# Gate and branch projections of a transformer layer as seven block products each, with tokens on the rows

## The reference

```python
h = rms_norm(x, norm1_g) * (1.0 + sc1) + sh1            # 256 x 1024
q1, q2, k1, k2, va, qs, ks, vs, ga, gb = split(h @ w_in)  # ga, gb: the last 2 x 1024 columns
oa = differential_attention(...)                        # 8 heads, normed per head
ob = stick_breaking_attention(...)                      # 16 heads of 64
merged = sigmoid(ga) * (oa @ w_pa) + sigmoid(gb) * (ob @ w_pb)
x = x + g1 * (merged @ w_o)
# then: norm, router, top 4 of 32 experts (SwiGLU, 1024 wide), final norm
```

## Time and profile before

| | |
|---|---|
| median of 3 runs | 1316.11 us |
| profiled execution, whole | 1315.63 us |
| its span in the trace | 1313.9 us |
| PE busy, share of the span | 1264.5 us, 96% |
| DVE busy | 551.4 us, 42% |
| ACT busy | 178.1 us, 14% |
| HBM read | 476.10 MB, 363 GB/s over the span |
| granted clock of PE, mean | 0.997 |

### The profile page before, as it was taken

One profiled execution on the slowest core, in us unless ns is written; L12 is line 12 of the kernel. 1 busy time (PEld: TensorE's weight loads), 2 busy tenths in 40 slices (PEclk: granted clock), 3 DMA queues, 4 the chain that ended last, 5 costly groups with the idle time before them and its releaser, 6 DMA issues.

```text
span 1313.9 us, 16916 instructions
## 1 busy us (share of the span) xinstructions
PE 1264.5 (96%) x5985; PEld 583.5 (44%) x5986; DVE 551.4 (42%) x1232; ACT 178.1 (14%) x378; POOL 12.6 (1%) x31
## 2 busy tenths in 40 slices
PE   6999999999999999999999999999999999899997
PEld 4867867888653333333333333333333333333332
DVE  3354695332253444434333343334344343334344
ACT  2102323320020110001100000001000111011002
POOL 0000000100000000000000000000000000000000
PEclk9999999999999999999999999999999999999999
DMA  9967665238669999999999999999999999799995
GB/s 354 331 248 273 246 236 203 77 128 324 256 228 413 430 429 427 428 430 427 428 430 428 428 429 429 427 428 429 410 430 427 427 430 428 315 429 430 429 427 208
DMA packets 59183, 477.55 MB, mean 363 GB/s; under 512 B 4991, under 2 KB 5076, under 8 KB 32532
## 3 DMA queue, kind: packets, MB, share of 16 engines
q1 hardware_dynamic: 58852, 476.11, 88.1%
q10 hardware_dynamic: 304, 1.06, 0.2%
HBM read 476.10 MB, written 1.05 MB: 363 GB/s over the span
## 4 chain that ended last, share of the span: by engine, by line
PE 75%; DMA 18%; DVE 4%; issue 1%; SPq 1%; ACT 0%; DVEq 0%
PE bank L1748 25%; DMA down_ring<-in_w_down 17%; PE bank L1787 15%; PE bank L1387 11%; PE bank L1580 4%; PE bank L1422 4%; PE bank L1736 3%; PE bank L1714 3%; PE bank L1636 2%; PE bank L1706 2%; PE bank L1478 1%; DMA down_ring<-in_w_ada 1%; DVE scratch L1208 1%; DVE scratch L1206 1%; DVE scratch L839 1%
## 5 line engine op out<-in xcount | busy, mean ns | idle before, releaser
L1748 PE MATMUL bank<-gu_ring,scratch 128*64 128x512 f32 x2048 | 459.3, 595 | 0.4 <-DVE scratch L1133 0.4
L1748 PEld LDWEIGHTS bank<-gu_ring,scratch 128*64 128x64 f32 x2048 | 143.3, 137 | 283.5 <-issue 283.2
L1787 PE MATMUL bank<-down_ring,scratch 128*64 128x512 f32 x1024 | 235.5, 602 | 23.0 <-DMA down_ring<-in_w_down 17.9
L1387 PE MATMUL bank<-gu_ring 128*128 128x256 f32 x640 | 143.8, 381 | 0.0
L1787 PEld LDWEIGHTS bank<-down_ring,scratch 128*64 128x64 f32 x1024 | 71.0, 137 | 145.4 <-issue 133.5
L1387 PEld LDWEIGHTS bank<-gu_ring 128*128 128x128 f32 x640 | 119.8, 190 | 20.3 <-issue 4.0
L1196 DVE TENSOR_TENSOR scratch<-bank,bgu 128x512 f32<-128x512 f32 x32 | 22.1, 691 | 219.1 <-PE bank L1714 219.1
L735 ACT ACTIVATE scratch<-bank 128x512 f32<-128x512 f32 x32 | 19.1, 597 | 683.2 <-PE bank L1748 683.2
L1164 DVE TENSOR_TENSOR xres<-xres,bank 128x512 f32<-128x512 f32 x132 | 81.8, 682 | 57.7 <-PE bank L1736 57.7
L1714 PEld LDWEIGHTS bank<-ident,scratch 128*128 128x128 f32 x392 | 41.0, 140 | 80.2 <-issue 26.7
L1132 DVE TENSOR_TENSOR scratch<-bank,a 128x256 f32<-128x256 f32 x66 | 27.8, 421 | 114.1 <-PE bank L1714 114.1
(11 more groups left out here) (271 smaller groups left out, 844.9 us busy)
## 6 DMA issues: line engine op xcount, KB each, us to landing
gu_ring<-in_w_gu SPq DMA_DIRECT2D x128, 2048.0 KB, 23.5
down_ring<-in_w_down SPq DMA_DIRECT2D x64, 2048.0 KB, 17.3
gu_ring<-in_w_in SPq DMA_DIRECT2D x32, 1024.0 KB, 8.5
gu_ring<-in_w_ada SPq DMA_DIRECT2D x16, 1024.0 KB, 7.1
down_ring<-in_w_ada SPq DMA_DIRECT2D x8, 512.0 KB, 10.5
gu_ring<-in_w_ada SPq DMA_DIRECT2D x8, 512.0 KB, 11.4
gu_ring<-in_w_pa SPq DMA_DIRECT2D x4, 1024.0 KB, 6.3
gu_ring<-in_w_pb SPq DMA_DIRECT2D x4, 1024.0 KB, 6.2
```

The costliest lines, as they stand in the source:

```text
L1387: last = M(dst[:, b * T:(b + 1) * T], group_chunk(group, kt // 4)[:, kt % 4, cols], hT[:, kt, :], start=kt == 0, stop=kt == KT - 1)
L1748: last = M(bank[f // 2][64 * a:64 * a + 64, :], xT[:, kt % 4, kt // 4, :], gu_ring[:, 8 * half + kt, f * 512:(f + 1) * 512], start=kt == 0 ...
L1787: last = M(bank[7][64 * a:64 * a + 64, :], act_sb[:, kt % 4, kt // 4, :], down_ring[:, kt // 2, (kt % 2) * D + a * 512:(kt % 2) * D + (a + ...
```

## The change

The four products are each made of seven block products, as the values are. `matrix(m, n)` is product `n` of matrix `m` (0 and 1 the gates, 2 and 3 the branches): 4 matmuls of 128 tokens by 512 columns. There are now 28 steps on PE, step `s` being `matrix(s // 7, s % 7)`, each followed by `stick_breaking(s)` while `s` is below 18. The results have the tokens on the rows. Sums of weight quarters (`sum_matrix`, four of 128x2048 for each matrix), sums of the left side for `oa` and `ob` (`sum_left`, four of 128x512 each; those of `h` are kept), and the additions of the products (`add_matrix`, five of 128x512 for each matrix) are written by hand into DVE's list between the `weigh` of the heads. ACT copies four blocks of each matrix from PSUM (`matrix_copy`) and applies the sigmoid later in place. The merged rows are turned by PE (`transpose_merged`, 8 transposes for each 128 tokens) and copied by ACT to `mergedT` before `mix`.

Product `n` waits for its sums, for copies that free its bank and for additions that have read it; the waits that matter are in the diff. On SP, both groups of a matrix come free together at its last product, and the loads for expert 1 into slots 8 to 15 come later and in another order.

```diff
-                    load_gu(1, 1, 0)
...
                 if j == 2:
-                    sp.wait_ge(merged_ready, 4)
-                    for pair in (2, 3):
-                        load_gu(1, 1, pair)
+                    sp.wait_ge(merged_ready, 2)
+                    load_gu(1, 1, 3)
+                    load_gu(1, 1, 0)
+                    sp.wait_ge(rowsT_done, 6)
+                    load_gu(1, 1, 2)
...
+            def matrix_copy(m, n):
+                act.wait_ge(product_done, 12 + 6 * m + (1, 3, 4, 4)[n])
...
+            def sum_matrix(m, n):
...
+                    last = V.tensor_tensor(first_sum[m], group_chunk(right, 0), group_chunk(left, 0), ALU.subtract)
+                elif n == 1:
...
+                    last = V.tensor_tensor(group_chunk(left, 0), group_chunk(right, 1), first_sum[m], ALU.subtract)
...
+            sum_matrix(0, 0)
+            dve.wait_ge(later_ready, 1)
+            weigh(0)
+            weigh(1)
+            add_matrix(0, 0)
...
+            sum_matrix(0, 1)
+            weigh(2)
+            weigh(3)
+            dve.wait_ge(root_ready, 2)
             own.then(V.reciprocal(osq[:], osq[:]))
             V.tensor_tensor(oav, oav, ...).then_inc(oa_ready, 1)
...
+            sum_matrix(0, 2)
+            add_matrix(0, 1)
+            add_matrix(0, 2)
+            weigh(4)
+            weigh(5)
+            obT_copy(0)
+            sum_matrix(0, 3)
+            add_matrix(0, 3)
+            weigh(6)
+            weigh(7)
+            obT_copy(1)
+            add_matrix(0, 4)
+            sum_matrix(1, 0)
+            add_matrix(1, 0)
+            weigh(8)
+            weigh(9)
+            obT_copy(2)
+            sum_matrix(1, 1)
+            sum_matrix(1, 2)
+            weigh(10)
+            weigh(11)
+            obT_copy(3)
+            add_matrix(1, 1)
+            sum_matrix(1, 3)
+            add_matrix(1, 2)
+            add_matrix(1, 3)
+            weigh(12)
+            weigh(13)
+            obT_copy(4)
+            add_matrix(1, 4)
+            sum_left(oaT)
+            sum_matrix(2, 0)
+            weigh(14)
+            weigh(15)
+            obT_copy(5)
+            obT_copy(6)
+            add_matrix(2, 0)
...
+            def matrix(m, n):
...
+                if n == 0:
+                    wait_group(pe, left, 0)
+                    if m == 0:
+                        pe.wait_ge(emptied, EMPTIED_HT + TURN_OAT)
+                        pe.wait_ge(parts_added, 6)
+                    elif m < 3:
+                        pe.wait_ge(parts_added, 10 + 5 * m)
+                    else:
+                        pe.wait_ge(obT_ready, SBH // 2)
...
+                if n == 2:
+                    pe.wait_ge(right_sums_ready, 8 + 4 * m + 1)
+                    if m < 3:
+                        pe.wait_ge(parts_added, 10 + 5 * m + 1)
...
+                if n == 3:
+                    pe.wait_ge(right_sums_ready, 8 + 4 * m + 2)
+                    pe.wait_ge(m_copied, 4 * m + 1)
...
+                if n == 6:
+                    pe.wait_ge(right_sums_ready, 8 + 4 * m + 4)
+                    pe.wait_ge(parts_added, 10 + 5 * m + 4)
+                for k in range(4):
+                    done = M(bank[into[m == 3]][:, :], rows_[:, k, :], cols[:, k, :], start=first and k == 0,
+                             stop=last and k == 3, skip_group_check=True)
...
+            for s in range(28):
+                if s == 5:
                     pe.wait_ge(oa_ready, 1)
+                    pe.wait_ge(parts_added, 13)
+                    transpose_oa(0)
...
+                if s == 27:
+                    pe.wait_ge(emptied, EMPTIED_HT + TURN_MERGED)
+                    transpose_merged(0)
+                matrix(s // 7, s % 7)
```

More of the change, by code:

```diff
@@ L612, in empty @@
                 branch, n = g // 6, g % 6
[L613 to L621, removed]
+                src = bank[(4, 6)[h] if g == 1 else turn % 2][:, :]
+                dst = qkT[:, branch, 4 * n + 2 * h:4 * n + 2 * h + 2, :].rearrange("p b t -> p (b t)")
+                A(dst, src, ACT.Copy, scale=DH ** -0.5 if n < 2 else 1.0).then_inc(emptied, 1)
             def differential(s):
@@ L673, in turned @@
                 A(sb_a[:, h % 3, :], bank[2 + h % 4][:, 0:384], ACT.Copy).then_inc(sbaT_ready, 1)
[L675 to L690, removed]
+            def matrix_copy(m, n):
+                act.wait_ge(product_done, 12 + 6 * m + (1, 3, 4, 4)[n])
+                tt, half = ((0, 0), (1, 1), (0, 1), (1, 0))[n]
+                A(gate_and_branch[m][:, tt, half * CW:(half + 1) * CW], bank[((0, 1, 0, 0), (2, 3, 2, 2))[m == 3][n]][:, :],
+                  ACT.Copy).then_inc(m_copied, 1)
@@ new lines, in gate_sigmoid, with oaT_copy @@
+            def gate_sigmoid(m, tt):
+                act.wait_ge(parts_added, 10 + 5 * m + 5)
+                A(gate_and_branch[m][:, tt, :], gate_and_branch[m][:, tt, :], ACT.Sigmoid).then_inc(sigmoid_ready, 1)
+            def oaT_copy(n):
+                act.wait_ge(rowsT_done, n + 1)
+                A(oaT[:, 2 * n:2 * n + 2, :].rearrange("p k t -> p (k t)"), bank[1][:, :], ACT.Copy,
+                  scale=nsub[:, 0:1]).then_inc(emptied, 1)
+            for s in range(28):
+                for n in {0: (0,), 2: (1,), 3: (2, 3)}.get(s % 7, ()):
+                    matrix_copy(s // 7, n)
+                for n in {5: (0, 1), 6: (2, 3)}.get(s, ()):
+                    oaT_copy(n)
+                if s in (8, 9, 15, 16):
+                    gate_sigmoid(s // 15, (s // 15 + s) % 2)
+                if s == 20:
@@ L699, in _ @@
                     keep_and_stop(s + 1)
+            for tt in range(TT):
+                for a in range(2):
+                    act.wait_ge(rowsT_done, 5 + tt)
+                    A(mergedT[:, 4 * a:4 * a + 4, tt * P:(tt + 1) * P],
+                      bank[(6, 4)[tt] + a][:, :].rearrange("p (k t) -> p k t", k=4), ACT.Copy).then_inc(emptied, 1)
             for tt in range(TT):
@@ new lines, in add_matrix @@
+            def add_matrix(m, n):
+                tt, half = ((0, 0), (1, 1), (0, 1), (1, 1), (1, 0))[n]
+                dst = gate_and_branch[m][:, tt, half * CW:(half + 1) * CW]
+                if n == 0:
+                    dve.wait_ge(product_done, 12 + 6 * m + 2)
+                    dve.wait_ge(m_copied, 4 * m + 1)
+                    other = bank[4 if m == 3 else 1][:, :]
+                elif n == 1:
+                    dve.wait_ge(m_copied, 4 * m + 3)
+                    other = gate_and_branch[m][:, 0, CW:2 * CW]
+                elif n == 2:
+                    dve.wait_ge(product_done, 12 + 6 * m + 5)
+                    dve.wait_ge(parts_added, 10 + 5 * m + 2)
+                    other = bank[3 if m == 3 else 1][:, :]
+                elif n == 3:
+                    dve.wait_ge(product_done, 12 + 6 * m + 6)
+                    dve.wait_ge(parts_added, 10 + 5 * m + 2)
+                    other = bank[5 if m == 3 else 0][:, :]
+                else:
+                    dve.wait_ge(filled, 2 * LAST_FILL[m] + 2)
+                    dve.wait_ge(m_copied, 4 * m + 4)
+                    other = bank[5 if m == 3 else 0][:, :]
+                V.tensor_tensor(dst, dst, other, ALU.add).then_inc(parts_added, 1)
@@ new lines, in obT_copy, with merge @@
+            def obT_copy(n):
+                dve.wait_ge(sbpv_done, 2 * n + 2)
+                V.tensor_copy(obT[:, n, :], bank[6 + n % 2][:, 0:T]).then_inc(obT_ready, 1)
+            def merge(n):
+                tt, half = ((0, 0), (0, 1), (1, 1), (1, 0))[n]
+                cols = slice(half * CW, (half + 1) * CW)
+                gate_b, branch_b, merged = gate_and_branch[1], gate_and_branch[3], gate_and_branch[0]
+                dve.wait_ge(parts_added, 25 + (1, 3, 4, 5)[n])
+                own.then(V.tensor_tensor(branch_b[:, tt, cols], branch_b[:, tt, cols], gate_b[:, tt, cols], ALU.mult))
+                last = V.tensor_tensor(merged[:, tt, cols], merged[:, tt, cols], branch_b[:, tt, cols], ALU.add)
+                if n % 2:
+                    last.then_inc(merged_ready, 1)
+                else:
+                    own.then(last)
@@ new lines, in gate_diagonals @@
+            def gate_diagonals(first):
+                for kt in range(KT):
+                    V.tensor_scalar(g1diag[:, kt, :], ident[:], mod[:, first + kt:first + kt + 1], None, ALU.mult
+                                    ).then_inc(diag_ready, 1)
+            dve.wait_ge(ada_summed, 2)
+            sum_matrix(0, 0)
[3 more added lines that the diff above has]
+            add_matrix(0, 0)
+            dve.wait_ge(cols_done, ADA_PARTS + 1)
+            own.then(V.tensor_tensor(mod[:, 16:48], bank[7][:, 16:48], vec[:, R_ADA + 16:R_ADA + 48], ALU.add))
@@ L988, in _ @@
             V.tensor_tensor(oav, oav, osq[:].unsqueeze(2).to_broadcast([P, 16, P]), ALU.mult).then_inc(oa_ready, 1)
[L989 to L1008, removed]
@@ new lines, in _ @@
+            gate_diagonals(M_G1)
+            sum_matrix(2, 2)
```

(34 more changed lines are left out.)

193 lines of the change are left out of this document (112 added, 81 removed).

## The result

The changed kernel takes 1321.71 us (median of 13 runs, 1319.9 to 1324.7) against 1317.03 us (13 runs, 1315.5 to 1320.9): a ratio of 1.0036, 95% interval 1.0028 to 1.0044. It is slower by 4.7 us. The profiled execution took 1319.9 us with a span of 1318.2 us, 4.3 us more than before. PE works less and the kernel is slower.

What follows compares the result with a forecast made beforehand. PE was taken to bound the rewritten stage. Its terms, -14.4 + 14.7 + 1.1 = +1.4 us, gave 1317.0 us for the profiled execution and about 1317.5 us for the median; range 1310 to 1323 us.

Steps and rivals of the forecast that it cites:

- the walk as it stands: Step-by-step walk through PE's and DVE's lists in the rewritten stage: 1317.5 us, 1314 to 1320; chance 0.48.
- rival A: PE's clock falls in step 7's wait, one product at half speed: +3.4 us, 1321 us; chance 0.30, including further slips.
- PE's saving: In the four products, 224 matmul records of 0.429 us replace 512 of 0.216 us: -14.4 us.
- The waits: PE waits for DVE at steps 2, 5, 6, 7, 10, 14 and 16 and before the router's shift: +14.7 us.
- The transposes: Sixteen transposes of merged rows on PE, the first eight standing where PE would wait anyway: +1.1 us.
- The clock: PE's clock holds through the rewritten stage's waits in the likeliest case: 0 us.
- Loads: Weight loads, some asked for later, stay hidden before mix and the first expert: costed at nothing.
- One to one to the end: A shift of the first expert shifts everything behind it by the same amount, up or down.
- B: DVE keeps up better in the rewritten stage, waits come to half, 7.4 us: time 1310 us; chance 0.17.
- C: Nothing waits in the rewritten stage, as busy shares suggest: 1302.8 us; chance 0.03.
- D: In the experts the stream of weights sets the end, so the shortening doesn't reach it: 1316 us; chance 0.02.
- The signs: Rewritten stage: waits sum to 12 to 19 us, longest about 5 us before step 7, mix within 3 us of 343.8.

Runs made afterwards that it cites:

- e3_order: Changed kernel with DVE's list reordered in five places, same work: 1307.62 us, ratio 0.9935 to the kernel before.
- e7_half_filled: Changed kernel with three wide matmuls put into PE's wait before step 7 and none before step 2: 1321.23 us, one run.
- e5_step2: Changed kernel with add_matrix(0, 0) moved ahead of weigh(0) in DVE's list: 1318.36 us, ratio 1.0010 to the kernel before.
- e6_filled_wide: Changed kernel with wide matmuls of 512 columns filling PE's waits, 2 before step 2 and 5 before step 7: 1318.48 us.

## Why the prediction was right and wrong, point by point

The time lies in the range, but not in the likeliest case: 1317.5 us was forecast as "the walk as it stands", no change, and rival A happened. The profiled execution was forecast at 1317.0 us and took 1319.9; the median is further off because that of the kernel before is 0.9 us higher in this group (1317.03 for 1316.11).

- **PE's saving** (-14.4 us): right. The products take 0.43 us a record, as the values did; the rewritten part of `e3_order`, nearly without waits, is 10.5 us shorter than before (128.95 for 139.40). That is the saving less the eight transposes ahead of step 27 (1.0 us), 2.0 us of waits and a rest of 0.9 us, which may lie at the changes between kinds of work; that is not shown.
- **The waits** (+14.7 us): right in their places, and 1.7 us too long in sum, 13.0 measured. Forecast and measured: step 2 2.7 and 2.5, step 5 0.9 and 0.6, step 6 0.8 and 0.7, step 7 5.2 and 5.1, step 10 2.5 and 2.2, step 14 0.9 and 0.65, step 16 1.4 and 1.2. The wait of 0.3 us before the shift did not show.
- **The transposes** (+1.1 us): too small. The first eight did not stand in a wait: the addition that step 27 needs had been made, and they cost 1.0 us; the second eight cost 0.9.
- **The clock** (0 us in the likeliest case): this is the step that failed. The prediction had the clock hold, and set the point from which rival A decides at "a wait of about 4 us on", from a single fall at the end of the trace. It fell in waits of 5.1, 2.5 and (in `e7_half_filled`) 2.3 us, as early as 2.1 us after PE's last work (`e5_step2`). `e6_filled_wide` prices the step: with both waits filled, the clock holds and 3.0 us of the rewritten part are gone. Rival A had the fall in step 7 alone, with a whole product at half speed for +3.4 us; there were two falls, each low for only part of a product, some 1.5 us each over the usual 3.6 to 3.7. That A's 1321 us fits is therefore partly luck. The Trainium skill, page "TensorE: Matmul & The Clock Gate", section "Why this matters for your kernels", advises against gaps of a few microseconds between bursts of matmuls. The falls in the 5.1 us waits agree with it; those at 2.5 and 2.3 us came in shorter gaps than the page warns of, and here the measurement decides.
- **The sum at the start of `mix`:** -14.4 + 13.0 + 3.1 + 1.0, and the rest of 0.9 us, make the 3.6 us measured. With 0.9 us for the second transposes, less 0.2 us behind them, it is the 4.3 us of the span. In the forecast the waits were 1.7 us too long, the transposes 0.8 us too short and this rest was left out: these errors cancel, which is luck, and what is left is the clock's 3.1 us.
- **Loads** (0 us): right. The second stage shows DMA at 0.95 for 0.75 before, and the first two experts wait for no load.
- **One to one to the end:** right. 13.6 us at `mix` gave 13.3 us at the end in `e3_order`.
- **Rivals B, C and D:** B had the waits at half and C had none; they came to 13.0 us. The order of DVE's list fixed them, as the prediction held against B. D is refuted by `e3_order`.
- **The signs:** the sum of the waits (13.0 us) lies in the 12 to 19 us that the prediction asked for, and the longest wait is where it was put. `mix` started 3.6 us later and not within 3 us; that too is the clock.

## What to carry to other kernels

Where an engine's list is in order, ask of every instruction what stands behind it and who waits for that, before counting busy shares: DVE, busy for 100 us in either order, cost PE 2.0 us of waits once five lines were moved, and 13.0 us with an instruction that had long been ready standing behind one that wasn't. Such waits can be worked out from the rows of the trace before, place by place, to a few tenths of a microsecond. Price a wait on PE of some 2.3 us or more with the low clock behind it, 1.5 to 2.3 us here, and not with its own length alone.

## What the runs showed of the hardware beyond what was expected

- PE's clock fell at every wait of 2.3, 2.5 and 5.1 us in the rewritten part and at none of 2.2 us. It was back in the course of the next product, so each fall cost 1.5 to 2.3 us (products of 5.13 to 5.94 us for 3.6). The longest wait was not the dearest by itself: behind 5.1 us the product took 5.13, 5.56 and 5.94 us in three traces, behind 2.5 us 5.20 to 5.37 in four.
- Two and five wide matmuls in the two waits, which left PE idle for 0.6 to 0.7 us, kept the clock at 1.00 and gained 3.2 us; three in the longer one, which left 2.3 us, didn't keep it.
- 27 small matmuls inserted into PE's list cost 6.1 us after the start of `mix`, with idle times of 1.6 and 4.7 us in the first two experts for which the profile names no releaser; 7 wide ones in the same places cost nothing there. The cause is open.
